# Hybrid SSD and DeltaNet layer on one core: the sums of squares of the state-space output by rounded high and low parts

## The reference, cut to what matters

```python
y = y.reshape(bsz, s, SSM_D_INNER) * jax.nn.silu(z)            # 1024 channels
yg = y.reshape(bsz, s, SSM_GROUPS, SSM_D_INNER // SSM_GROUPS)  # 2 groups of 512
yg = yg * lax.rsqrt(jnp.mean(yg * yg, axis=-1, keepdims=True) + EPS)
```

## Time and profile before

| | |
|---|---|
| median of 3 runs | 2468.01 us |
| the profiled execution's own time | 2469.87 us |
| its span | 2468.1 us |
| PE busy | 2384.2 us, 97% |
| DVE busy | 1708.3 us, 69% |
| POOL busy | 1368.6 us, 55% |
| ACT busy | 888.4 us, 36% |
| granted TensorE clock, mean | 0.989 |

### The profile page before, as it was taken

The page is one execution under the profiler, slowest core; times in us unless marked ns, Lnnn a source line. Parts: engine busy times, 40 slices in busy tenths (PEclk is TensorE's granted clock), DMA queues, the critical chain, the costliest instruction groups (busy, mean ns, idle before and its releaser), DMA issues. The chain is left out here.

```text
span 2468.1 us, 29891 instructions
## 1 busy us (share of the span) xinstructions
PE 2384.2 (97%) x11396; PEld 1964.4 (80%) x11396; DVE 1708.3 (69%) x1535; ACT 888.4 (36%) x1065; POOL 1368.6 (55%) x747
## 2 busy tenths in 40 slices
PE   7999999899999999989999899999999999999998
PEld 6888888677778888878878678888888888878776
DVE  4987999335774656743334887677676788999986
ACT  5234443545513233431014544334333333433332
POOL 2336887545544454533363265565565557897663
PEclk9999999999999999999999999999999999999999
DMA  6232334687674757554242222222222342232432
GB/s 225 88 94 89 116 103 152 200 283 267 219 244 151 229 173 234 185 172 170 75 146 84 87 71 84 85 85 68 102 76 76 103 162 77 102 119 87 139 114 96
DMA packets 260123, 335.35 MB, mean 136 GB/s; under 512 B 44766, under 2 KB 205867, under 8 KB 253867
## 3 DMA queue, kind: packets, MB, share of 16 engines
q1 hardware_dynamic: 181786, 279.81, 33.4%
q10 hardware_dynamic: 78224, 54.01, 6.9%
HBM read 230.50 MB, written 103.28 MB: 135 GB/s over the span
## 5 line engine op out<-in xcount | busy, mean ns | idle before, releaser
L495 POOL TENSOR_SCALAR w_hi<-w_raw 128x1024 fp32r<-128x1024 f32 x99 | 118.7, 1199 | 552.0 <-issue 478.9
L510 PE MATMUL ps<-act_hi,w_hi 128*128 128x512 f32 x944 | 383.4, 406 | 7.0 <-ACT ring_b L1231 2.5
L514 PE MATMUL ps<-act_hi,w_lo 128*128 128x512 f32 x944 | 368.6, 390 | 0.0
L513 PE MATMUL ps<-act_lo,w_hi 128*128 128x512 f32 x944 | 368.1, 390 | 0.0
L497 POOL TENSOR_TENSOR w_lo<-w_raw,w_hi 128x1024 fp32r<-128x1024 f32 x99 | 273.9, 2767 | 8.3
L2173 POOL TENSOR_TENSOR w_lo<-sm,w_hi 128x512 fp32r<-128x512 f32 x120 | 209.0, 1743 | 116.4 <-ACT w_hi L2578 116.4
L2173 POOL TENSOR_TENSOR w_lo<-w_raw,w_hi 128x512 fp32r<-128x512 f32 x90 | 138.9, 1545 | 152.4 <-ACT w_hi L2578 152.4
L510 PEld LDWEIGHTS ps<-act_hi,w_hi 128*128 128x128 f32 x944 | 177.7, 188 | 47.7 <-issue 6.2
L513 PEld LDWEIGHTS ps<-act_lo,w_hi 128*128 128x128 f32 x944 | 177.8, 188 | 38.1 <-issue 4.1
L514 PEld LDWEIGHTS ps<-act_hi,w_lo 128*128 128x128 f32 x944 | 177.3, 188 | 37.8
L2311 PE MATMUL ps<-t,w_hi 128*128 128x512 f32 x480 | 187.1, 390 | 0.2 <-POOL w_lo L2173 0.2
(11 more groups left out here) (421 smaller groups left out, 5871.7 us busy)
## 6 DMA issues: line engine op xcount, KB each, us to landing
w_raw<-in_w_in_dram SPq DMA_DIRECT2D x34, 1024.0 KB, 6.4
kept_c<-ring_a ACTq DMA_DIRECT2D x36, 512.0 KB, 3.2
w_raw<-in_w_ffn_down_dram SPq DMA_DIRECT2D x18, 1024.0 KB, 5.0
w_raw<-in_w_ffn_up_dram SPq DMA_DIRECT2D x16, 1024.0 KB, 5.2
w_raw<-in_w_ffn_gate_dram SPq DMA_DIRECT2D x16, 1024.0 KB, 5.2
f_cm<-ring SPq DMA_DIRECT2D x32, 512.0 KB, 2.6
dn_raw<-f_cm SPq DMA_DIRECT2D x24, 512.0 KB, 4.4
qkv_a<-kept_c SPq DMA_DIRECT2D x7, 1536.0 KB, 6.8
```

The costliest lines, as they stand in the source:

```text
L495: nc.gpsimd.tensor_scalar(hi, raw, 1.0, 0.0, ALU.mult, ALU.add).then_inc(split_done, 1)
L510: first = nc.tensor.matmul(o, wh, mov[0][:, k, c], start=(k == 0), stop=False)
L513: nc.tensor.matmul(o, wh, mov[1][:, k, c], start=False, stop=False)
L514: last = nc.tensor.matmul(o, wl, mov[0][:, k, c], start=False, stop=(k == KD - 1))
```

## The change

The sums are computed from two rounded parts. ACT's square of `yssm` is written as `ysq_hi` in float32r, and no longer waits for the reduction of the DeltaNet squares (`o_ssq`). DVE gets two instructions more: `sqs = yssm * yssm` in float32, placed ahead of `scale_x`, and `ysq_lo = sqs - ysq_hi` in float32r, placed between `scale_x` and `invert_x`. TensorE's 8 products of 128x128 in float32 become 8 products of 128x256 in float32r, 4 of `ysq_hi` and 4 of `ysq_lo`, each over both groups at once (`k:KD:4` picks tile k and tile k + 4). They wait for the second DVE instruction. `ysq_hi` lies where `ysum` is, and `ysq_lo` where `sqs` is; `ones` keeps its place and is read in float32 elsewhere.

```diff
@@ allocations
-    ones = sb("ones", [P, P])
+    ones_r = sb("ones", [P, P], f32r)
+    ones = ones_r[:, :].bitcast(f32)
...
+    sub = ExitStack()
+    ysq_hi = sb("ysq_hi", [P, KD, P], f32r, sub)
+    ysq_lo = sb("ysq_lo", [P, KD, P], f32r, sub)
+    sub.close()
     ysum = sb("ysum", [P, D_MODEL], f32, ph2)
     sqs = sb("sqs", [P, KD, P], f32, ph2)
...
+    ysq_split = a_qk
@@ pe_mixer main
-            after(pe, ysq_done, c + 1)
-            for g in range(SSM_GROUPS):
-                for k in range(4):
-                    last = t.matmul(bank(PC)[:, g * P:(g + 1) * P], ones[:, :], sqs[:, 4 * g + k, :], start=(k == 0), stop=(k == 3))
+            after(pe, ysq_split, 2 * NCH + 2 * c + 2)
+            sums = bank(PC)[:, 0:SSM_GROUPS * P].rearrange("p (g t) -> p g t", g=SSM_GROUPS)
+            for k in range(4):
+                t.matmul(sums, ones_r[:, :], ysq_hi[:, k:KD:4, :], start=(k == 0), stop=False)
+                last = t.matmul(sums, ones_r[:, :], ysq_lo[:, k:KD:4, :], start=False, stop=(k == 3))
@@ act_mixer main
-            after(act, o_ssq, c + 1)
-            a(sqs[:, :, :], yssm[:, :, :], ACT.Square).then_inc(ysq_done, 1)
+            a(ysq_hi[:, :, :], yssm[:, :, :], ACT.Square).then_inc(ysq_done, 1)
@@ dve_mixer main
             v.tensor_tensor(yssm[:, :, :], yssm[:, :, :], zt[:, :, :], ALU.mult).then_inc(y_mid, 1)
+            after(dve, y_mid, c * 2 + 2)
+            after(dve, o_ssq, c + 1)
+            v.tensor_tensor(sqs[:, :, :], yssm[:, :, :], yssm[:, :, :], ALU.mult).then_inc(ysq_split, 1)
             if more:
                 scale_x(c + 1)
+            after(dve, ysq_done, c + 1)
+            after(dve, ysq_split, 2 * NCH + 2 * c + 1)
+            v.tensor_tensor(ysq_lo[:, :, :], sqs[:, :, :], ysq_hi[:, :, :].bitcast(f32), ALU.subtract).then_inc(ysq_split, 1)
+            if more:
                 invert_x(c + 1, 0)
                 invert_x(c + 1, 1)
```

## The result

The changed kernel takes 2490.2 us (2487.13 to 2492.3, four runs) against 2468.2: the ratio is 1.0086, with a 95% interval of 1.0073 to 1.0099. It is slower by 22 us, where 12.4 had been forecast. The profiled execution has a span of 2488.6 us, 20.5 more than before.

What follows compares the result with a forecast made beforehand. PE's order of work was taken to set the time. Chunk gains of 1.8 us less losses of 14.2 made a loss of 12.4 us: 2480.4 against the median (2482.3 against the profiled execution), range 2469 to 2490.

Steps and rivals of the forecast that it cites:

- PE's saving: In each chunk's sums, 8 float32r records take 0.98 us instead of 1.88; a chunk with nothing late gains 0.9 us.
- Turns at the port: After the product with `zt`, the new square waits for GpSimd's whole mask in chunks 3, 4, 6: losses 1.9, 5.0, 4.95 us.
- The rival in which such a square is free: A square of one tile read twice doesn't collide; the subtraction waits for GpSimd's mask: loss 5.7 us, 2474; chance 0.12.
- the one in which DVE keeps its turn: DVE runs two dependent instructions without yielding; GpSimd's mask then catches the subtraction: loss 9.3 us, 2477.5; chance 0.07.
- DVE ahead of `decayed_x`: Behind `scale_x`, DVE's subtraction should go before GpSimd's `decayed_x`, so no wait for it was priced.
- Chunk 5: GpSimd is done when the product with `zt` ends; the corner product moves from 1001.38 to 1003.0: loss 1.6 us.
- shift with: The next chunk's loads, issued behind PE's and DVE's steps, are delayed along with them; priced at nothing.
- Waits of 5 us: PE idle ahead of the sums by 5 to 6 us in chunks 4 and 6, released by DVE.
- The clean chunks: Chunks 0 and 2: in chunk 2 `xinv` is ready before the sums start, chunk 0 is alike; each gains 0.9 us.
- `decayed_x` first: GpSimd's `decayed_x` gets ahead of the subtraction and holds it for 1.9 us: about 10 us more, 2490; chance 0.07.

Runs made afterwards that it cites:

- the second trace: The whole change, unaltered, executed and traced again: 2491.97 us, the median of two executions (2486.86 and 2497.07); the trace is of the slower one.
- products in the wait: The whole change plus unused 128x512 products before TensorE's wait for the sums, 18 in chunks 4, 5 and 6, 12 in chunk 7: 2484.34 us, ratio 1.0055.

## Why the prediction was right, and where it was off

- **PE's saving** was right to the record: eight products in 1.03 us in chunk 0 (0.98 forecast), at 0.118 us each (0.122). The value was taken from the streamed columns and not from the spacing of 512-column records, and held.
- **Turns at the port**, and that a square of one tile read twice takes part: right, and the step that carries the result. The square is 5.47, 5.45 and 5.46 us in chunks 3, 4 and 6, the chunks named, and 1.23 in 0, 1 and 2. Moving the mask (2473.5 us) and cutting it (2472.3) show it as the cause, with DVE's work left whole. The forecast's sentence on the rule of the Trainium skill (SBUF — State Buffer, "Who interferes with whom"), which counts inputs and not tiles, is borne out by these rows. The rival in which such a square is free, at 2474 us, is out, as is the one in which DVE keeps its turn. (The 0.03 us by which DVE's dependent instruction follows stands in the earlier trace rows, and not in the earlier trace rows as the forecast says; the value holds, 959.98 to 960.01 in chunk 4.)
- **DVE ahead of `decayed_x`**: right in all seven chunks where both occur (2.76 us for a GpSimd instruction of 1.91).
- **Chunk 5** failed: "POOL is done" took the landing of `dec` from one trace as fixed. It landed 2.8 us later, and the chunk cost 5.8 us instead of 1.6, which is 4.2 of the missing 7.6 us. The square ended 33.07 us after the start of the chunk where the forecast had 30.72: that is 2.35 us of turns at the port, and the clock behind the longer wait is the other 1.8. The sentence that the loads "shift with" the steps is half right. The load of `dec` is issued 14.98 us after the start of chunk 5 before, after and in the second trace, but it lands 5.2, 7.9 and 6.2 us behind that.
- **The clock** was left out of the sum, and is the largest part of the miss. Waits of 5 us were forecast, and what follows them was priced at the high level. From the end of the subtraction to the transposes of `qs` it takes 4.69 us at the high level (chunk 4 with products in the wait), and 6.33, 6.51 and 6.83 us in chunks 4, 5 and 6 of the change: 1.6, 1.8 and 2.1 us. Only the first is shown by an experiment in the same chunk; for the other two the rows have the same low-level distances. In chunks 4 and 6 it was offset in part, as `dec` landed 0.9 and 1.4 us earlier in the chunk than before, so the misses there are only 0.7 and 0.8 us.
- **The clean chunks** 0 and 2: the gain of 0.9 us was priced with the delay of `decayed_x` and the splits at nothing, because their users come in the next chunk. The users weren't the question. The split holds the port when the scaling of `qs` comes. That cost 1.3 and 0.7 us, shown by delaying the splits.
- The sum was 12.4 us, the spans differ by 20.5, and the medians by 22. At 2490.2 the time lies on the very end of the range (2490), and that is luck: the end had been set by a rival that did not happen (`decayed_x` first), while the terms that brought the time there, the clock and the landing in chunk 5, were in no sum and in no rival. Direction and mechanism were right; the size was short by close to half.

## What to carry to other kernels

Where VectorE and GpSimd both read two tiles from SBUF, count each VectorE instruction as a turn: a second one right behind the first hands the port to whatever GpSimd has waiting, for the whole of that instruction. Long GpSimd instructions beside a chain on the critical path are best cut or put behind it, and the delayed ones have to be followed until they have met every later VectorE instruction of that kind. A wait of several microseconds on TensorE can cost, besides its own length, the slow work behind it (1.6 us behind 5.1 here), and a meeting that hangs on when a load lands needs both outcomes in the range.

## What the runs showed of the hardware

- After 5.1 us without products the granted clock was 0.66 on the mean of 10 us; products of 128x256 in float32r followed at 0.213 us instead of 0.118, and 16 records of 64 columns took 1.97 us instead of 1.15. The length of the wait alone does not tell the level: behind 3.77 us in chunk 7 the eight products of the change still followed at about 0.12 us and the gemm step after them slowed, while with the mask moved, behind the same 3.77 us, the products themselves followed at 0.213.
- The same kernel, executed twice, had the load of `dec` land at 23.8 and at 25.4 us after the start of chunk 1, and at 22.9 and 21.1 in chunk 5. By the turns at the port the square took 1.23 or 5.48 us in chunk 1, and 5.45 or 1.23 in chunk 5. The chunks differed by less, 2.6 and 0.7 us, since the product with `zt` waits where the square does not.
- Four instructions of 128x512 on GpSimd take 4.04 us where one of 128x2048 takes 3.61, so cutting cost 0.4 us, and no time in the kernel before (ratio 0.9988).
